# Swapping the scale of one unit and the maximum of the next in VectorE's order of an attention pipeline

## The reference, cut to what matters

```
s = (q @ k.T) * scale, masked
m = max(s)                      # with the sink, where there is one
p = exp(s - m)
p = p / sum(p)                  # with exp(sink - m), where there is one
o = p @ v
```

## Time and profile before

| | us |
|---|---|
| median of 3 runs | 2609.9 (2609.86 to 2615.91) |
| the profiled execution's own time | 2609.84 |
| its span, first to last instruction | 2608.0 |
| PE busy in the span | 2409.2 (92%) |
| DVE busy | 1369.4 (53%) |
| ACT busy | 923.9 (35%) |
| mean granted TensorE clock | 0.962 of full speed |

### The profile page before, as it was taken

How to read it: one execution, slowest core, us unless ns; L and a number is a source line. 1 busy time by engine, 2 the same in 40 slices (tenths; PEclk the granted TensorE clock), 3 DMA queues, 4 the chain that set the end, 5 groups by cost and what they waited for, 6 DMA issues and landing times.

```text
span 2608.0 us, 30433 instructions
## 1 busy us (share of the span) xinstructions
PE 2409.2 (92%) x11732; PEld 1872.0 (72%) x11732; DVE 1369.4 (53%) x1633; ACT 923.9 (35%) x1365; POOL 281.2 (11%) x188
## 2 busy tenths in 40 slices
PE   7988989999998889999998799999996789999997
PEld 6765557887876557887876567888875546788886
DVE  5446875664545565664536654333355655433333
ACT  4324653443323353442323343322225453332221
POOL 0000003110013003110000013110140000311010
PEclk9987999999999899999998899999998789999999
DMA  4310002222222102222222202222321101222231
GB/s 168 129 65 1 1 1 77 100 96 84 96 96 89 65 1 81 96 96 97 97 97 89 81 24 88 99 85 92 113 89 65 38 27 36 87 104 82 96 109 68
DMA packets 31204, 202.54 MB, mean 78 GB/s; under 512 B 4356, under 2 KB 5256, under 8 KB 7432
## 3 DMA queue, kind: packets, MB, share of 16 engines
q1 hardware_dynamic: 29816, 198.14, 21.5%
q10 hardware_dynamic: 1296, 3.15, 0.4%
HBM read 199.17 MB, written 2.10 MB: 77 GB/s over the span
## 4 chain that ended last, share of the span: by engine, by line
PE 81%; DVE 13%; ACT 4%; issue 2%; DMA 0%; ACTq 0%; DVEq 0%; SPq 0%
PE D L522 69%; PE X L594 3%; PE D L615 2%; PE D L607 2%; DVE neg_max L1593 2%; DVE w_lo L1402 2%; DVE xg L1427 1%; ACT w_hi L958 1%; PE X L599 1%; ACT prob L1116 1%; DVE mid L1402 1%; ACT mid L958 1%; PE X L560 1%; DVE h L1442 1%; DVE prob_t L1619 0%
## 5 line engine op out<-in xcount | busy, mean ns | idle before, releaser
L522 PE MATMUL D<-xg,w_hi 128*128 128x512 f32 x3184 | 992.8, 393 | 51.5 <-DVE xg L1427 29.4
L522 PE MATMUL D<-mid,w_hi 128*128 128x512 f32 x2312 | 731.7, 398 | 23.0 <-DVE w_lo L1402 9.2
L522 PEld LDWEIGHTS D<-xg,w_hi 128*128 128x128 f32 x3184 | 601.2, 189 | 182.8 <-DVE w_lo L1402 23.8
L1402 DVE TENSOR_TENSOR w_lo<-w_raw,w_hi 128x2048 fp32r<-128x2048 f32 x184 | 451.2, 2452 | 381.7 <-ACT w_hi L958 380.9
L522 PE MATMUL D<-xg,w_lo 128*128 128x512 f32 x1592 | 623.7, 392 | 0.0
L522 PEld LDWEIGHTS D<-mid,w_hi 128*128 128x128 f32 x2312 | 435.1, 189 | 134.1 <-issue 17.4
L958 ACT ACTIVATE w_hi<-w_raw 128x2048 fp32r<-128x2048 f32 x184 | 351.6, 1911 | 501.3 <-PE D L522 493.9
L522 PE MATMUL D<-mid,w_lo 128*128 128x512 f32 x1156 | 458.7, 397 | 0.0
L522 PEld LDWEIGHTS D<-xg,w_lo 128*128 128x128 f32 x1592 | 301.3, 189 | 63.6
L522 PEld LDWEIGHTS D<-mid,w_lo 128*128 128x128 f32 x1156 | 218.3, 189 | 53.0
L1442 DVE TENSOR_TENSOR h<-D,h 128x1024 f32 (+1 forms) x72 | 88.0, 1222 | 283.2 <-PE D L522 283.2
(11 more groups left out here) (233 smaller groups left out, 1815.7 us busy)
## 6 DMA issues: line engine op xcount, KB each, us to landing
w_raw<-in_weights SPq DMA_DIRECT2D x184, 1024.0 KB, 4.8
h<-in_x SPq DMA_DIRECT2D x4, 512.0 KB, 7.8
out_y<-h SPq DMA_DIRECT2D x4, 512.0 KB, 2.7
inv_cnt<-in_inv_cnt ACTq DMA_DIRECT2D x1, 1024.0 KB, 4.8
cos<-in_cos ACTq DMA_DIRECT2D x3, 256.0 KB, 5.2
sin<-in_sin ACTq DMA_DIRECT2D x3, 256.0 KB, 5.8
vec<-in_vec SPq DMA_DIRECT2D x1, 262.0 KB, 2.7
cos<-in_cos_m ACTq DMA_DIRECT2D x1, 256.0 KB, 2.7
```

Of the source, the lines that this page charges most:

```text
L522: last = nc.tensor.matmul(out, w[a], x[b], start=start and k == 0, stop=stop and k == 2)
L1402: return nc.vector.tensor_tensor(out, x, f(high), ALU.subtract)
```

## The change

In DVE's `attend`, the block with the maximum of unit s is moved behind the block with the scale of unit s-1 (with its sink write) and stays ahead of the copy of unit s-2. No instruction is added or removed. PE's, ACT's and SP's programs stay as they are.

```diff
                 for s in range(count + 4):
-                    if s < count:
-                        a = a0 + s
-                        c, w = 2 * (a % 2), len(key_blocks(kind, units[s][1])) * P + (kind in SINK0)
-                        dve.wait_ge(scored, a + 1)
-                        nc.vector.tensor_reduce(neg_max[:, c:c + 2], X[:, c:c + 2, 0:w], AX_X, ALU.max,
-                                                negate=True).then_inc(maxed, 1)
                     if 0 <= s - 1 < count:
                         a = a0 + s - 1
...
                                 ins = nc.vector.tensor_scalar(p, p, inv, None, ALU.mult)
                         ins.then_inc(normed, 1)
+                    if s < count:
+                        a = a0 + s
+                        c, w = 2 * (a % 2), len(key_blocks(kind, units[s][1])) * P + (kind in SINK0)
+                        dve.wait_ge(scored, a + 1)
+                        nc.vector.tensor_reduce(neg_max[:, c:c + 2], X[:, c:c + 2, 0:w], AX_X, ALU.max,
+                                                negate=True).then_inc(maxed, 1)
                     if 0 <= s - 2 < count:
```

## The result

The changed kernel takes 2672.4 us (median of 4 runs, 2670.9 to 2673.7). The kernel before took 2610.5 (median of 4 runs, one of them on the same chip as the changed kernel). The ratio is 1.0234, with a 95% interval of 1.0219 to 1.0249: slower by 62 us. The forecast was 2665, in a range of 2657 to 2676.

What follows compares the result with a forecast made beforehand. PE came near to setting the pace in all four attention stages; a closed DVE-ACT chain would replace it. Stage terms of +31.7, +19.2 and +4.3 gave +55.2 on 2609.84, so 2665 us, range 2657 to 2676.

Steps and rivals of the forecast that it cites:

- The closed chain: DVE and ACT in attention: maximum, exponential, scale, next maximum without overlap; 2.91 us a unit in `nsa`, against 2.56.
- The tile ends: DVE's subtraction waits for ACT's copy inside the chain: +1.09 us each, 7 in `nsa`, 8 in `swa` and `even`, 2 in `odd`.
- PE's part at a change of tile: In `nsa`, the transpose and copy path delays the second exponential: estimated +0.3 us at 7 tile changes, +2.1.
- PE's start at half clock: At the start of `nsa`, PE's pace rules over four short units instead of the chain: +0.7 us.
- The stages: First to last maximum: `nsa` 193.1 us (+31.7), `swa` and `even` 126.8 (+19.2), `odd` 58.0 (+4.3).
- The rest: Fill before first maxima, tails and projections: taken as 0, with at most 2 us saved over four tails.
- the rival of the clock: PE's new gaps bring 1.2 GHz back inside the stages, +24 us over the forecast, 2689; chance 0.08.
- the slack swallows it: DVE's idle time, 30 us in `nsa` alone, absorbs the new order at no cost: 2610 us; chance 0.02.
- the swap helps PE: DVE's copy follows the maximum at once, transposes stop waiting and 20.2 us come back: 2590 us; chance 0.02.
- The idle time ahead of the reciprocal: Sign on DVE: no row before; should be among the large ones and be ended by ACT's exponential.
- Idle time ahead of the maxima: Sign on DVE: 62.8 us before, should nearly vanish because the scores lie ready.
- ACT's waits: Sign on ACT: waits for `neg_max` should grow to about scale + maximum a unit.

Runs made afterwards that it cites:

- The added wait: Kernel before, with the maximum of each unit also waiting for the exponential of the unit before: 2615.8 us, ratio 1.0004.
- the copy in the chain: Changed kernel with DVE's copy of unit s-2 moved ahead of the maximum of unit s (order scale, copy, maximum): 2722.1 us.
- the late split: Changed kernel with DVE's subtraction at each tile end, except the last tile's, moved one step on, right behind the next unit's maximum: 2651.2 us.
- the extra PE work: Changed kernel with the first head's score product of every unit done twice, the first result being overwritten: 2687.8 us.
- the late split on the kernel before: Kernel before with DVE's subtraction at tile ends moved one step on, behind the next unit's maximum: 2614.8 us, ratio 1.0003.
- the fourth order: Kernel before with its last two DVE pieces swapped (maximum of unit s, copy of s-2, scale of s-1): 2625.1 us, ratio 1.0038.

## Why the prediction was right, point by point

**The closed chain** held. Its length per unit, taken from four handovers and three durations, was 3.85 for width 4 in `nsa`, and 3.85 was measured. The steady unit of `odd` was put at 3.72 and measured 3.73 (2192.47 to 2196.20 in DVE's timeline). In a steady tile of `nsa` the distances from one maximum to the next are 2.01, 2.30, 2.63, 3.70, 3.24, 3.24, 3.85 and 3.85, two for each width. Without the two terms below, the second and the fourth would be 2.01 and 2.62, and a unit costs 2.93 on average, where the sum had 2.91. The added wait, the copy in the chain and the late split each moved the time by what the chain gives to the piece that they touch.

**The tile ends**, +1.09 each, held: the fourth distance has 1.08 more than its twin, and the late split took 1.07 or 1.08 a tile out again.

**PE's part at a change of tile**, an estimate of 0.3, measured 0.29 (2.30 against 2.01), and for the reason given: the maximum ends at 267.97, but ACT's copy of the unit of width 4, which waits for PE's transpose, comes first, and the exponential starts at 268.30. The prediction calls the copy that ends at 298.10 one of width 4; it has 384 columns, which is width 3. The number stands all the same, for what takes the time is the transpose behind it, of width 4: in the changed kernel the exponential follows the end of DVE's copy (266.56) by the same 1.74. PE's start at half clock, taken at +0.7, cost 0.9: the fourth distance of the first tile is 3.53, with a wait of 0.82 for PE's scores.

**The stages.** Predicted 193.1, 126.8 and 58.0; measured 195.0, 127.0 and 58.1. Their sum was 2.2 us short: +55.2 against +57.4, nearly all of it in `nsa`. Of its 1.9, about 1.0 is the unit at 2.93 instead of 2.91, 0.2 the start, and 0.7 one tile that took 25.52 instead of 24.82, with the granted clock at 0.80 from 288.80 to 296.00.

**The rest.** This is the part that the prediction missed. The profiled runs differ by 63.9 us in span, and 6.5 of these lie outside the stages: 4.0 between `nsa` and `swa`, 0.9 between `swa` and `even`, 1.6 behind the last maximum. The sum had 0 there, and that is why the time came out near the upper end of the range. The 4.0 can be seen. The next windows are of the end of `nsa`, first in the changed kernel, then before:

```profile
411.31:428.00 16.69, 12.32 (x74) 10.17 (x75) 4.83 (x9) 3.24 (x7) 0.00 (x0) 0.70 0.00 1
```

```profile
377.68:395.00 17.32, 14.23 (x111) 11.57 (x112) 5.90 (x12) 3.74 (x10) 0.00 (x0) 1.00 0.00 1
```

In the changed kernel the clock was at 0.70 over the end of `nsa`, where it was at 1.00 before. The last transposes and products of the stage took nearly twice as long, 2.5 us more together (again the changed kernel first):

```profile
415.99 1.94 PE L607 MATMUL D<-ident,prob 128*128 128x128 f32 x8 [0.74 <-DVE prob_t L1619]
417.86 3.68 PE L615 MATMUL D<-prob_t,vall 128*64 128x128 f32 x32
```

```profile
382.60 1.06 PE L607 MATMUL D<-ident,prob 128*128 128x128 f32 x8
383.59 2.04 PE L615 MATMUL D<-prob_t,vall 128*64 128x128 f32 x32
```

So the rival of the clock, which had 0.08, was there in a small part: single short falls worth a few microseconds, not the 24 us of a clock that swings. But the traces do not tie these falls to the chain. The stretch between the last maximum of `nsa` and the first of `swa` took 518.7 us here and 514.7 before. With the same chain in `nsa` it took 513.4 with the swap in `nsa` only, 513.4 with the extra PE work and 513.1 with the late split; with the late split on the kernel before, which has no chain, it took 517.6. Over the first 20 us of it the granted clock was 0.74 in the changed kernel, but 0.91, 1.00 and 1.00 in those three kernels with the chain. So a few microseconds of this stretch differ from one execution to another.

Nor does the clock inside the stages follow the chain. In `swa` it stands at 0.93 before, with PE busy 90%, at 0.87 with 83% in the changed kernel, and at 0.79 with 79% with the copy in the chain as well; but with the late split it stands at 0.98, and PE is busy only 81%. In `even` it was 0.88 before and 0.97 after. No run changed the clock alone, so its share of the 6.5 us, and what makes it fall, stay open.

**The rivals.** That the slack swallows it fell with the result, and again with the copy in the chain. That the swap helps PE fell too: the copy did come right behind its maximum (309.31), and transposes waited 69 us, not less, because they now wait for a later maximum.

**The signs named ahead.** The idle time ahead of the reciprocal was to be large: it is 62.9 us, and 28.7 more ahead of the sink writes, ended by ACT. Idle time ahead of the maxima was to vanish nearly: 11.0 us are left. ACT's waits were to reach about scale and maximum a unit: 178.9 us over 128 units is 1.4, against about 1.7 from the earlier trace rows; ACT's own copies, 0.44 each, lie in that time. The clock was to stay over 0.9 inside the stages: it did in three, and was 0.87 in `swa`. The prediction called a clock under 0.9 a sign of its clock rival. It was a poor sign, for `even` stood at 0.88 before the change. In `swa` it did little to the length: its tiles took 10.74 or 10.75, apart from the first (9.67, which holds no tile end) and one of 11.05.

## What to carry to other kernels

In a hand-written pipeline over engines, look for what stands *behind* each wait in an engine's queue, and follow it until it closes on itself. One swap of two blocks that look independent closed a cycle over two engines, and the cycle's length became the period. Whether that costs anything is one comparison: the cycle against the present period, 2.91 + tile ends against 2.56 here. A block that moves also takes along what it signals to others, as the sink write in the fourth order did. Wait and work need to be told apart: the wait alone, with a shorter cycle, was nearly free. Work that lies beside the cycle is free as well, until it is queued inside it.

## What the runs showed of the hardware that was not expected

Waits and instructions add up with great regularity. Handovers of 0.03 to 0.04 us between DVE and ACT and an overlap of 0.08 between neighbours on DVE, read at a few places, gave `swa` and `even`, together 127 us, to within 0.2. What did not repeat was TensorE's granted clock. The same projections between two stages took 513.1 to 518.7 us from one profiled kernel to another, and the runs of the kernel before lay between 2609.6 and 2616.8 us.
